# Gate products moved in front of the last unit of a chunked RWKV-7 recurrence, with scores, key transposes and key loads reordered

## The reference, cut to what matters

```
g = sigmoid(x_g @ g1) @ g2                       # output gate, (512 x 128) @ (128 x 1024)
y = scan(r, decay, k, v, kk, a) forward + scan(...) backward   # per head of 64
y = head_norm(y) * lnx_g + lnx_b + bonus
x = x + (y * g) @ w_out                          # (512 x 1024) @ (1024 x 1024)
h = rms_norm(x); logits = h @ router_w; softmax; top 64 tokens of each expert
out = rms_norm(x + sum over experts of silu(h Wg) * (h Wu) @ Wd, weighted and scattered)
```

## Time and profile before

| | |
|---|---|
| profiled execution | 1578.85 us, span 1577.1 us |
| median of three runs | 1578.98 us |
| TensorE busy | 1467.5 us, 93% |
| VectorE busy | 512.4 us, 32% |
| mean DMA rate | 317 GB/s |
| recurrence, units 0 to 7 | 270 to 537 us of the span |
| mix_output | 538 to 637 us |
| experts | 638 to 1577 us |

### The profile page before, as it was taken

One profiled execution on the slowest core, in us unless ns is written; L12 is line 12 of the kernel. 1 busy time (PEld: TensorE's weight loads), 2 busy tenths in 40 slices (PEclk: granted clock), 3 DMA queues, 4 the chain that ended last, 5 costly groups with the idle time before them and its releaser, 6 DMA issues.

```text
span 1577.1 us, 25943 instructions
## 1 busy us (share of the span) xinstructions
PE 1467.5 (93%) x11404; PEld 737.5 (47%) x11404; DVE 512.4 (32%) x725; ACT 240.7 (15%) x488; POOL 179.7 (11%) x349
## 2 busy tenths in 40 slices
PE   7999999888897898999999989989989989989996
PEld 6344445888887655434334324324324324324332
DVE  6666634667665555101101101101201201201113
ACT  3334311212221121100000000000000000000002
POOL 1323503433232120000000000000000000000000
PEclk9999999999999999999999999999999999999998
DMA  9245577766755653699999999999999999999995
GB/s 306 67 160 167 181 280 173 157 161 136 144 101 104 247 237 160 241 428 427 428 433 431 426 434 431 427 431 433 431 428 432 435 426 433 433 426 436 420 425 218
DMA packets 172502, 500.46 MB, mean 317 GB/s; under 512 B 125776, under 2 KB 134992, under 8 KB 152960
## 3 DMA queue, kind: packets, MB, share of 16 engines
q1 hardware_dynamic: 166624, 479.30, 78.4%
q0 software_dynamic: 5792, 19.89, 3.7%
HBM read 470.84 MB, written 28.33 MB: 317 GB/s over the span
## 4 chain that ended last, share of the span: by engine, by line
PE 44%; DMA 12%; DVE 2%; issue 1%; ACT 1%; DVEq 0%; SPq 0%
PE pD L1652 13%; PE pU L1622 11%; DMA ring<-in_exp_w_up 10%; PE pG L1622 9%; PE pG L1595 5%; PE pX L1583 4%; DMA ring<-in_exp_w_down 2%; DVE res L1770 1%; DVE hid L1790 1%; PE pX L1633 1%; PE pD L1595 0%; ACT xin L1711 0%; PE pX L1671 0%; DVE res L1808 0%; ACT hidT L1728 0%
## 5 line engine op out<-in xcount | busy, mean ns | idle before, releaser
L1790 DVE TENSOR_TENSOR hid<-silu,pU 128x512 f32<-128x512 f32 x32 | 20.6, 684 | 737.4 <-PE pU L1622 737.4
L1622 PE MATMUL pU<-ring,xin 128*64 128x512 f32 x768 | 177.2, 617 | 26.4 <-DMA ring<-in_exp_w_up 26.4
L1622 PE MATMUL pG<-ring,xin 128*64 128x512 f32 x768 | 169.7, 594 | 6.4 <-DMA ring<-in_exp_w_gate 5.4
L1652 PE MATMUL pD<-ring,hidT 128*64 128x512 f32 x768 | 168.1, 593 | 2.3 <-ACT hidT L1728 2.1
L1622 PEld LDWEIGHTS pU<-ring,xin 128*64 128x64 f32 x768 | 55.9, 142 | 146.0 <-issue 106.8
L1595 PE MATMUL pG<-yexp,scatter 128*128 128x512 f32 x232 | 112.8, 618 | 3.4 <-DVE res L1770 1.9
L1652 PEld LDWEIGHTS pD<-ring,hidT 128*64 128x64 f32 x768 | 55.3, 137 | 108.3 <-issue 106.4
L1622 PEld LDWEIGHTS pG<-ring,xin 128*64 128x64 f32 x768 | 53.6, 137 | 110.2 <-issue 102.0
L1770 DVE TENSOR_TENSOR res<-res,pG 128x512 f32<-128x512 f32 x116 | 78.8, 686 | 43.8 <-PE pG L1595 43.7
L1595 PEld LDWEIGHTS pG<-yexp,scatter 128*128 128x128 f32 x232 | 37.0, 188 | 78.8 <-DVE res L1770 55.1
L1583 PEld LDWEIGHTS pX<-pick,y 128*128 128x128 f32 x512 | 61.0, 199 | 6.6 <-issue 4.2
(11 more groups left out here) (250 smaller groups left out, 1772.2 us busy)
## 6 DMA issues: line engine op xcount, KB each, us to landing
ring<-in_exp_w_down SPq DMA_DIRECT2D x18, 4096.0 KB, 25.8
ring<-in_exp_w_gate SPq DMA_DIRECT2D x18, 4096.0 KB, 31.5
ring<-in_exp_w_up SPq DMA_DIRECT2D x18, 4096.0 KB, 25.1
ring<-in_exp_w_gate SPq DMA_DIRECT2D x12, 2048.0 KB, 24.0
ring<-in_exp_w_up SPq DMA_DIRECT2D x12, 2048.0 KB, 19.2
ring<-in_exp_w_down SPq DMA_DIRECT2D x12, 2048.0 KB, 23.5
lent_slot<-in_exp_w_gate SPq DMA_DIRECT2D x6, 4096.0 KB, 28.7
lent_slot<-in_exp_w_down SPq DMA_DIRECT2D x6, 4096.0 KB, 30.9
```

The costliest lines, as they stand in the source:

```text
L1622: mm = pe.matmul(psum[f // 2][HEAD * s:HEAD * s + HEAD, :], xin[:, k, e, :], w[:, FF * r + HALF * f:FF * r + HALF * f + HALF], start=k == ...
L1652: mm = pe.matmul(pD[h][HEAD * s:HEAD * s + HEAD, :], hidT[:, j, c, HEAD * s:HEAD * s + HEAD], w[:, k, HALF * h:HALF * h + HALF], start=j = ...
L1790: dve.tensor_tensor(hid[:, j, :], silu[:, j, :], pU[j][:, :], ALU.mult).then_inc(hid_done, 1)
```

## The change: what it does

Four things.

1. The eight gate products move from `mix_output` to `recurrence`, on TensorE in front of unit 7 (`output_gates`), through the two pS banks; ScalarE copies each to SBUF (`gates`), between the Square and the Sqrt of the head norm. In `mix_output` VectorE multiplies y by them out of SBUF. g2 is loaded at the start of the recurrence rather than at its end. A 16 KB per partition buffer `scores_or_gates` holds the gates, and before them an input mix and the scores SC2, after them four small buffers of `experts`.
2. In a unit, TensorE transposes the keys behind the first two fills rather than behind the two levels; the scores of unit n + 2 each move up by one or two steps, the decays too. VectorE makes the four key products of unit n + 2 earlier, in front of or between the level masks, and masks the scores before it adds the state.
3. SyncE issues the keys of unit n + 3 before it waits for the scores of unit n + 2.
4. In `mix_output`, `turn_res(t - 1)` uses banks of its own and comes directly behind `turn(t)`; weight block 3 waits for the last logits as well, since `resT` now lies in its slot.

```diff
+def output_gates():                       # TensorE, in front of unit LAST
+    pe.wait_ge(keep["g2_load"], 16)
+    pe.wait_ge(tk_ev, 4 * LAST)
+    for i in range(2 * TILES):
+        t, h = i // 2, i % 2
+        if i >= 2:
+            pe.wait_ge(keep["gate_ev"], i - 1)
+        pe.matmul(pS[h], gate_low[tile t], g2[half h]).then_inc(keep["gate_mm"], 1)

 # ScalarE, n == LAST
-    head_norm_roots(act, keep, 0)
+    act.wait_ge(y_mm, 2 * LAST)
+    gates(0, 3)
+    head_norm_squares(act, keep, 0)
+    gates(3, 5)
+    head_norm_root(act, keep, 0)
+    gates(5, 2 * TILES)

 # TensorE, unit n
     fill(n, 0, 0, scored(n), of(X))
+    turn_keys(n, (0, 1))
     fill_with_values(n)
+    turn_keys(n, (2, 3))
     for g in range(2):
         fill(n, 2 + g, g, of(XT[n % 2]), of(W))
         fill(n, g, g, of(W), of(XT[n % 2]))
-        turn_keys(n, (2 * g, 2 * g + 1))
 ...
     sum_r(n, 1)
+    scores(n + 2, 0)
     sum_state(n, 0)
     sum_y_state(n, 0)
+    scores(n + 2, 1)
     sum_r_state(n, 1)
-    scores(n + 2, 0)
     sum_y_state(n, 1)
-    scores(n + 2, 1)
+    scores(n + 2, 2)
     solve_u(n, 1)
-    scores(n + 2, 2)
+    scores(n + 2, 3)
     sum_state(n, 1)
-    scores(n + 2, 3)
+    cumulate(n + 3, (0, 1))
     sum_y(n, 0)
-    cumulate(n + 3, (0, 1))
+    cumulate(n + 3, (2, 3))
     sum_y(n, 1)
-    cumulate(n + 3, (2, 3))

 # VectorE, unit n
     for g in range(2):
         add_to(n, X, g, 2 + g, 3 + 2 * g)
         add_to(n, XT[n % 2], g, g, 4 + 2 * g)
+        removed_keys(n + 2, g)
-    removed_keys(n + 2, 0)
+    added_keys(n + 2, 0)
     for g in range(2):
         cross(n, 1, g, 2 + g, 7 + g)
+    added_keys(n + 2, 1)
     for g in range(2):
         add_to(n, XT[n % 2], g, g, 9 + g)
-    removed_keys(n + 2, 1)
     removed(n, 0)
-    added_keys(n + 2, 0)
+    masked(n + 2, 0)
     add_state(n, 0)
-    added_keys(n + 2, 1)
-    masked(n + 2, 0)
     masked(n + 2, 1)
+    masked(n + 2, 2)
     removed(n, 1)
-    masked(n + 2, 2)
+    masked(n + 2, 3)
     add_state(n, 1)
-    masked(n + 2, 3)

 # SyncE
     inverses(n + 1)
+    load_keys(n + 3)
     blocks(n + 2)
-    load_keys(n + 3)

 # mix_output, TensorE, tile t
     turn(t)
-    gate(t + 1)
+    turn_res(t - 1, 0); turn_res(t - 1, 1)
     project(t, 0)
-    turn_res(t - 1, 0); turn_res(t - 1, 1)
     project(t, 1)
     logits(t - 1)
```

More of the change, by code:

```diff
@@ L344, in _ @@
                 act.wait_ge(norm_max, t + 1)
[L345 removed]
+                act.activation(stat[:, 1, t:t + 1], stat[:, 2, t:t + 1], ACT.Sqrt).then_inc(norm_root, 1)
             for c in range(DC):
@@ L779, in projected, with gates @@
                     act.activation(v_stage[t][:, at:at + HALF], pT[k % 2][:, :], ACT.Copy).then_inc(v_ev, 1)
+            def gates(first, end):
+                for i in range(first, end):
+                    act.wait_ge(keep["gate_mm"], i + 1)
+                    act.activation(keep["gates"][:, TILE_ORDER[i // 2], HALF * (i % 2):HALF * (i % 2) + HALF], pS[i % 2][:, :],
+                                   ACT.Copy).then_inc(keep["gate_ev"], 1)
             decays(0)
@@ L999, in _ @@
                 sum_r(n, 1)
+                if ahead:
+                    scores(n + 2, 0)
                 for e in range(2):
@@ L1336, in _ @@
         def _(pe):
-            def gate(t):
-                for h in range(2):
-                    if t:
-                        pe.wait_ge(gated, 2 * (t - 1) + h + 1)
-                    pe.matmul(ps[h][:, :], keep["gate_low"][:, P * TILE_ORDER[t]:P * TILE_ORDER[t] + P], g2[:, HALF * h:HALF * h + HALF],
-                              start=True, stop=True).then_inc(gate_mm, 1)
             def turn(t):
                 for g in range(2):
+                    pe.wait_ge(gated, 2 * t + g + 1)
                     for c in range(4):
@@ L1372, in logits @@
                     mm.then_inc(logit_mm, 1)
-            pe.wait_ge(keep["g2_load"], 16)
-            gate(0)
             for t in range(TILES):
-                pe.wait_ge(gated, 2 * t + 2)
-                if t >= 2:
-                    pe.wait_ge(turn2_ev, 2 * (t - 1))
+                if t:
+                    pe.wait_ge(turn1_ev, 2 * t)
                 turn(t)
-                if t + 1 < TILES:
-                    gate(t + 1)
+                if t:
+                    for g in range(2):
+                        turn_res(t - 1, g)
                 pe.wait_ge(turn1_ev, 2 * t + 2)
@@ L1386, in _ @@
                 project(t, 0)
-                if t:
-                    for g in range(2):
-                        turn_res(t - 1, g)
                 if t < TILES - 1:
@@ L1510, in experts @@
         gated_pick = sb("gated_pick", P, TILES, 2, CAP)
-        scatter = sb("scatter", P, 2, SEQ)
+        hidT = sb("hidT", P, 2, 4, P)
         xin = sb("xin", P, DC, 2, CAP)
-        silu = sb("silu", P, 2, HALF)
-        hid = sb("hid", P, 2, HALF)
-        hidT = sb("hidT", P, 2, 4, P)
-        yexp = sb("yexp", P, D)
+        scatter, silu, hid = (keep["gates"][:, k, :].rearrange("p (j f) -> p j f", f=HALF) for k in range(3))
+        yexp = keep["gates"][:, 3, :]
         pG, pU, pD, pX = ([ctx.enter_context(nc.psum_tensor(f"{n}{i}", [P, HALF], F32)) for i in range(2)] for n in ("pG", "pU", "pD", "pX"))
```

54 lines of the change are left out of this document (32 added, 22 removed).

## The result

The changed kernel takes 1593.18 us in the median of four runs (1592.57 to 1594.12), the kernel before 1577.7 in four of the same day (1575.39 to 1579.17): ratio 1.009, 95% interval 1.0069 to 1.0111. It is slower by 15.5 us in the medians and 14 by the ratio (11 to 18). The forecast was 1569.3 with a range from 1560 to 1576, and 0.05 for slower. One execution of the kernel of experiment 6 took 4209.84 us and counts in no ratio.

The account below looks back on a forecast made before the run. The experts' 940 us are bound by weight transfers, but their stream starts only after the choice of tokens, so earlier gains shift the end. Units -3.0 and mix_output -6.5 give -9.5 from 1578.85: 1569.3 us, range 1560 to 1576.

Parts of the forecast that it names:

- the way from the last mask to the first fill is 36.4 us: Mask to first fill two units on: 36.4 us, 35.5 covered, so a 0.9 us wait stays of 2.24 before unit 6.
- Unit 0: Units 0 to 4 priced alike: a clean unit becomes 33.7 us against 32.7, +1.0 each.
- The mid-unit wait: Inside a unit, TensorE waits 2.1 us, from 10.9 to 13.05, before the second level for VectorE's masks.
- VectorE's new order decides: Rival, chance 0.07: two more key products before the second level delay the solve in six units; 1583.4 us, slower.
- In front of unit 7: Gate products replace TensorE's wait; unit 7's fill starts 8.55 us behind unit 6 instead of 6.78: +1.8.
- Unit 7: With the clock kept up, unit 7 takes 24.3 us against 29.4, including 1.0 for issue stalls: -5.1.
- The rival on the clock: Rival, chance 0.09: the clock stays at 1.2 GHz in front of unit 7, which stays at 29.4; 1574.4 us.
- mix_output: Earlier start -2.7, shorter tile periods -3.9, last tile -0.8, VectorE's lateness +0.9; taken -6.5 us.
- the port rival: Rival, chance 0.10: GpSimd and VectorE block each other in mix_output's tiles 2 and 3; 1574.0 us, rather 1572.
- The end follows: Gains before the first choice of tokens shift the weights' stream and the end by as much; contrary rival 0.04, 1579 us.

Follow-up runs that it names:

- experiment 6: Changed kernel with all key transposes at their old place and SyncE's queue as before; 1579.94 us, 0.9993 of the kernel before.
- experiment 1: Changed kernel with the units' order on TensorE, VectorE and SyncE as before, so only gates and mix_output changed; 1576.18 us, 0.9979 of the kernel before.
- experiment 2: Changed kernel with only the keys' loads put back behind the blocks in SyncE's queue; 1586.37 us, 1.0044 of the kernel before.
- 3: Kernel before with one edit: SyncE issues the keys of unit n + 3 in front of the blocks of unit n + 2; 1587.99 us, 1.0046.
- 4: Kernel before with the keys' loads issued between the store of the scores and the load that waits for it; 1582.48 us, 1.0011.
- 8: Kernel of experiment 6 with one key product moved behind the second level's masks; 1574.73 us, 0.996 of the kernel before.
- 12: Kernel of 8 plus four unread TensorE products around mix_output's first turn and an early Sqrt on ScalarE; 1573.98 us, 0.9955 of the kernel before.
- 5: Changed kernel with the transposed keys of unit 0 alone at their old place; 1588.18 us, 1.0049 of the kernel before.
- experiment 9: Kernel of experiment 1 plus four products nobody reads, two before and two behind mix_output's first turn; 1573.83 us, 0.9963 of the kernel before.
- 11: Kernel of experiment 9 plus a small Sqrt on ScalarE before its wait for unit 6, loading the table early; 1575.29 us, 0.9958 of the kernel before.

## Why the prediction was wrong, step by step

The ratios split the loss: gates and `mix_output` -3.3 us (experiment 1), the order of scores, keys and masks +2.2 (6), the transposes in front +8.1 (2 against 6), the keys' loads first +7.3 (after against 2). Each term is uncertain by some 3 to 4 us; the two large ones are clear of zero, the 2.2 is not.

**The failed step: "the way from the last mask to the first fill is 36.4 us".** The prediction took this way as fixed and used it for slack alone. The same edit that it credited with taking waits away (keys "go out before the scores are waited for") stands in that way. The queue is in order: when the masks are done, two loads are issued first, behind inverses that are late themselves, and the store then takes 2.5 us longer to come back (unit 3; up to 3.7 in the others). With the way at 36.4 only the fill of unit 6 should have waited, 0.9; with ways like the 44.3 of unit 3, each unit from 2 to 6 waits 1.5 to 5.0, 14.6 together. The prediction followed the moved scores and transposes past everything that they pass on TensorE, and did not do so for the moved loads on SyncE. Shown by 3, where this edit alone costs 7 us, and by 2, where undoing it gives 7 us back; 4 leaves open how much of it is the place in front of the store and how much the transfers themselves.

**The second: GpSimd in the same way.** GpSimd's chain for one unit takes about 14.7 us before, 16.0 after and 16.9 in experiment 2, with the same instructions. VectorE and GpSimd in order of time, kernel after:

```profile
355.23 1.22 DVE L1065 TENSOR_TENSOR BK<-lent_slot 64x1024 f32<-64x1024 f32 x1
355.29 1.28 POOL L736 TENSOR_TENSOR XB<-XB,step_sum 128x28 f32<-128x28 f32 x1
356.46 1.22 DVE L1069 TENSOR_TENSOR BK<-lent_slot 64x1024 f32<-64x1024 f32 x1
356.64 1.15 POOL L733 TENSOR_TENSOR step_sum<-NB,XB 128x39 f32<-128x39 f32 x1
357.61 1.27 DVE L1100 TENSOR_TENSOR W<-pI,con 128x512 f32<-128x512 f32 x2
357.87 0.27 POOL L736 TENSOR_TENSOR XB<-XB,step_sum 128x39 f32<-128x39 f32 x1
358.22 0.27 POOL L733 TENSOR_TENSOR step_sum<-NB,XB 128x48 f32<-128x48 f32 x1
358.57 0.28 POOL L736 TENSOR_TENSOR XB<-XB,step_sum 128x48 f32<-128x48 f32 x1
358.91 1.22 DVE L1069 TENSOR_TENSOR BK<-lent_slot 64x1024 f32<-64x1024 f32 x1
358.93 1.36 POOL L733 TENSOR_TENSOR step_sum<-NB,XB 128x55 f32<-128x55 f32 x1
```

An operation of 0.27 us takes 1.15 to 1.36 when it starts beside a key product (both inputs in SBUF) and 0.27 beside a mask (one input in PSUM). From 255 to 515 us, of some 232 such operations, 20 are lengthened before, 18 in experiment 1, 28 in 6, 29 after and 33 in experiment 2, each by about 0.9 us. All 20 and all 29 started beside a VectorE product of two SBUF inputs (18 and 24 of them key products, the rest queries and decays), and of the other 415 only 3 did. By the Trainium skill, SBUF — State Buffer, section SBUF: two separate sides, a VectorE operation with two SBUF inputs that starts first locks a GpSimd operation that reads SBUF out for the whole instruction. The traces agree: the lengthened operations end 0.07 to 0.27 us behind the product's end. The prediction named this rule for `mix_output` and not for the stage where GpSimd sits in the path that sets the units' start. Each of the 24 key products of units 2 to 7 now lengthens one of GpSimd's operations; before, 18 did. What this costs the whole is not shown: in experiments 3, 8 and 12 all 24 do so too, and 8 and 12 are faster than the kernel before.

**Unit 0 (+5.7, priced at +1.0).** The prediction treated five units alike. Unit 0 has a dependence of its own, the store of the values from TK, and the transposes were moved in front of its end. Shown by 5.

**The mid-unit wait (2.1 us) was right** in units 1 to 5: 1.6 to 2.2 us each, with 0.7 in unit 0. The rivals' chances were not: of the five, the one with 0.07, "VectorE's new order decides", gave the sign but not the cause, since its place is worth only 2 of 17 us, and even these are not clear of the noise. No rival had the inverses' way. This is the same error again: a round trip over two queues and an engine was read as one number.

**In front of unit 7: right.** Gaps of 0.34 and 0.52 us, fill 8.6 us behind unit 6 (8.55 forecast). In experiment 1, 31.9 us from fill to fill against 30.05: +1.8, as forecast. In the kernel after it is 33.4, since unit 6 starts behind its wait at a granted clock of 0.60 (493.88 to 498.00) and takes 24.8 us instead of 23.3.

**Unit 7: 28.3 (27.8 in experiment 1), forecast 24.3.** The clock did stay at 1.00 through gates and start (after, 520 to 540). But the stalls of issue (0.78 at 534.37 and 2.22 at 540.63, 2.35 in experiment 1, priced at 1.0) came back, and behind them the granted clock fell, to 0.66 from 540 to 545 in after, to 0.66 from 520 to 525 in experiment 1, a mean between 1.2 and 2.4 GHz. In experiment 1 these two are the whole difference: its unit 7 takes 4.5 us longer than its unit 6, 2.35 of them the stall and some 2 the products behind it at the lower clock. The rival on the clock came nearly true, not at the unit's start but by its other ground, the stall of issue that returns. So 1.0 to 1.6 us of the forecast 5.1 came.

**mix_output: -2.6, forecast -6.5.** The start is right: projection 3.7 us behind the unit's end, where it was 6.4, thus -2.7. But without the gate products TensorE waits 1.79 and 0.69 there, and the first projection takes 16.98 instead of 13.90 us. The two waits alone don't decide it: the same two stand in experiments 1 and 8, with 14.00 behind them. The first period is 18.8 for 16.4 before. Later periods are 18.2 and 17.6 (17.4 forecast). VectorE and GpSimd do meet, in the way of the port rival: VectorE waits 2.31 us at 568.53 for a GpSimd operation, itself 3.39 long beside VectorE's product at 565.00, but the `turn` at 576.20 doesn't wait for it; and in the period of 18.2 a VectorE operation of 0.17 us takes 2.22 at 586.95, beside a GpSimd operation from 586.80 on, and the `turn` at 594.36 waits 0.63. Experiment 9's products go with 13.90 us in each of three kernels; that they gain time is not clear of the noise (0.9963 against 0.9979).

**The end follows**: right, within 1.3 us.

## What to carry to other kernels

Before an issue is moved in an in-order queue, write down every round trip that passes through that queue and what then stands in front of its store; a load "that is early anyway" belongs behind the store that somebody waits for. A dependence chain through several engines is not a constant: list who shares ports and queues with each of its links, and price the first iteration by itself. Ask how much slack the chain has: here a way that grew by 4.4 us cost nothing that could be told, one that grew by 5.9 cost 7 (experiments 4 and 3). Where products are removed, look at the granted clock behind the place where they stood: here the first projection ran in part at the lower level in six of eight kernels without them.

## What the runs showed of the hardware that was not expected

- A store issued behind two bulk loads in the same queue came back 2 to 4 us later (7.1 to 8.7 us from issue to the dependent load, against 4.9 to 5.1), beside the 2 us that the loads' own issue took. With the loads issued between the store and its dependent load it was 6.0 to 7.4 us.
- GpSimd operations of 0.27 us beside a VectorE product of 1.22 us with both inputs in SBUF take 1.15 to 1.36: 49 of 49 lengthened ones in two traces stood beside such a product.
- TensorE stalls 0.5 to 2.8 us in unit 7, laid to issue, at places of its program that are 127 or 128 products apart (once twice that) and the same in all traces within one product, whatever stands there, each time until 1.2 to 1.6 us behind the end of a 16 KB transfer of instructions. It does so with or without the w_out load beside it. The granted clock falls behind it in some traces (experiments 1 and 6, after) and not in others (1.00 behind a stall of 1.68 in experiment 9 and of 2.83 in 11).
